# Cutting the attention output of a head pair in two halves of 512 queries on GpSimd

## What is computed

```python
def fox_attend(q, k, v, cq, ck, q_pos, k_pos):
    s = jnp.einsum('bqhd,bkhd->bhqk', q, k) * (1.0 / math.sqrt(HEAD_DIM))
    decay = cq_transposed[..., :, None] - ck_transposed[..., None, :]
    s = jnp.where(mask, s + decay, -inf)
    p = jax.nn.softmax(s, axis=-1)
    return jnp.einsum('bhqk,bkhd->bqhd', p, v)

o = attend(q).reshape(B, T, D_MODEL)
h = h + o @ w_o[l]
h = h + sq_relu_mlp(h, g_mlp[j], w_up[j], w_down[j])
```

## Time and profile before

| | |
|---|---|
| median of 3 runs | 2430.94 us (2430.47 to 2437.22) |
| the profiled execution | 2431.78 us, span 2430.0 us |
| TensorE busy | 2277.4 us, 94% of the span |
| VectorE busy | 1083.5 us, 45% |
| ScalarE busy | 584.0 us, 24% |
| GpSimd busy | 607.9 us, 25% |
| attention of the prompt | about 1290 to 1580 us from the span's start |
| output projection | 1580 to 1672 us |
| last MLP | 1672 us to near the end |

### The profile page before, as it was taken

The page is one execution under the profiler, slowest core; times in us unless marked ns, Lnnn a source line. Parts: engine busy times, 40 slices in busy tenths (PEclk is TensorE's granted clock), DMA queues, the critical chain, the costliest instruction groups (busy, mean ns, idle before and its releaser), DMA issues. The chain is left out here.

```text
span 2430.0 us, 35893 instructions
## 1 busy us (share of the span) xinstructions
PE 2277.4 (94%) x14058; PEld 2081.0 (86%) x14058; DVE 1083.5 (45%) x1757; ACT 584.0 (24%) x1257; POOL 607.9 (25%) x416
## 2 busy tenths in 40 slices
PE   3179999999999999999999999899999999999998
PEld 2179999999999996777776666699999999999997
DVE  5874343343343376544125777734424324334331
ACT  3142011011011043333214666622201101101101
POOL 1053223222322351210000110245223322322331
PEclk6589999999999999999998999999999999999999
DMA  4011111111111122544337454311111111111112
GB/s 122 0 30 44 52 45 44 45 53 44 45 47 49 37 86 83 174 137 122 132 131 185 110 121 98 78 35 44 52 45 44 47 51 44 44 47 50 44 44 80
DMA packets 194086, 169.14 MB, mean 70 GB/s; under 512 B 28560, under 2 KB 168896, under 8 KB 193927
## 3 DMA queue, kind: packets, MB, share of 16 engines
q1 hardware_dynamic: 152985, 136.92, 19.5%
q10 hardware_dynamic: 40950, 30.02, 3.9%
HBM read 136.77 MB, written 30.50 MB: 69 GB/s over the span
## 5 line engine op out<-in xcount | busy, mean ns | idle before, releaser
L322 PE MATMUL ps<-xn_hi,w_lo 128*128 128x352 f32 x1584 | 515.5, 325 | 62.8 <-DVE h L1859 39.4
L322 PE MATMUL ps<-xn_lo,w_hi 128*128 128x352 f32 x1584 | 510.1, 322 | 0.0
L322 PE MATMUL ps<-xn_hi,w_hi 128*128 128x352 f32 x1584 | 509.8, 322 | 0.0
L551 PE MATMUL ps<-hid_hi,w_lo 128*128 128x352 f32 x1536 | 495.4, 323 | 0.0
L551 PE MATMUL ps<-hid_lo,w_hi 128*128 128x352 f32 x1536 | 492.7, 321 | 0.0
L551 PE MATMUL ps<-hid_hi,w_hi 128*128 128x352 f32 x1536 | 492.2, 320 | 0.0
L300 POOL CAST w_hi<-w_raw 128x1024 fp32r<-128x1024 f32 x138 | 144.8, 1049 | 1136.3 <-issue 529.4
L621 DVE TENSOR_TENSOR h<-ps,h 128x352 f32<-128x352 f32 x384 | 198.3, 522 | 446.4 <-PE ps L551 446.4
L589 ACT ACTIVATE tmp_b<-tmp_a 128x352 f32<-128x352 f32 x192 | 95.3, 498 | 1090.6 <-DVE tmp_a L607 1090.6
L322 PEld LDWEIGHTS ps<-xn_hi,w_lo 128*128 128x128 f32 x1584 | 299.1, 189 | 66.5 <-DVE xn_lo L1853 39.6
L302 POOL TENSOR_TENSOR w_lo<-w_raw,w_hi 128x1024 fp32r<-128x1024 f32 x138 | 332.8, 2412 | 11.1
(11 more groups left out here) (211 smaller groups left out, 2489.1 us busy)
## 6 DMA issues: line engine op xcount, KB each, us to landing
w_raw<-in_w_up SPq DMA_DIRECT2D x64, 512.0 KB, 4.0
w_raw<-in_w_down SPq DMA_DIRECT2D x64, 512.0 KB, 3.4
out<-tok_out ACTq DMA_DIRECT2D x32, 256.0 KB, 2.2
qk_dram<-turn_hi ACTq DMA_DIRECT2D x32, 256.0 KB, 2.4
qk_dram<-turn_lo ACTq DMA_DIRECT2D x32, 256.0 KB, 2.9
k_page<-in_cache_k SPq DMA_DIRECT2D x32, 256.0 KB, 3.3
v_page<-in_cache_v SPq DMA_DIRECT2D x16, 512.0 KB, 9.0
q_a<-qk_dram SPq DMA_DIRECT2D x32, 256.0 KB
```

The lines of the kernel that those rows point to most:

```text
L322: last = pe.matmul(ps[:, bank, 0:CH], w, x(k, c), start=(k == 0 and i == 0), stop=(k == nk - 1 and i == 2))
L551: last = pe.matmul(ps[:, NC * (dm % 2) + c, 0:CH], w, x, start=(k == 0 and i == 0), stop=(k == GT - 1 and i == 2))
```

## The change

A pair is cut in two halves of 512 queries. `cut_o_pair(r, g)` waits until both heads have their half g in `oT`: 8 r copies of the pairs before, and 6 of this pair for the first half (two halves of the first head, one of the second) or 8 for the second. Each half raises `o_cut` by two, so pairs now raise it by 4, and all cuts together by 34. Chunk 0 of the first block of the projection reads columns 0 to 351 only, and waits ahead of k for the first half of pair k. Chunk 1 waits once for all cuts. The two weight splits stay ahead of pair 7.

```diff
                         elif par == 0 and c == 0:
-                            before = lambda k: pe.wait_ge(o_cut, 2 + 2 * (k + 1))
+                            before = lambda k: pe.wait_ge(o_cut, 2 * (2 * k + 1) + (2 if k else 0))
+                        elif par == 0 and c == 1:
+                            pe.wait_ge(o_cut, 4 * NP + 2)
                         last = products(pe, par, 0, KT, c, NC * par + c, oh, ol,
...
-            def cut_o_pair(r):
-                pool.wait_ge(o_ev, 8 * (r + 1))
-                cut_o(r + 1 if r else 0, r, slice(0, T))
-
-            cut_o_pair(0)
+            def cut_o_pair(r, g):
+
+                pool.wait_ge(o_ev, 8 * r + 6 + 2 * g)
+                cut_o(2 * r + g + (1 if r else 0), r, slice(512 * g, 512 * g + 512))
+
+            cut_o_pair(0, 0)
+            cut_o_pair(0, 1)
             pool.wait_ge(s_oc, 16)
             pool.tensor_copy(o_hi[:, :, T:N], o_s[:, :, :]).then_inc(o_cut, 1)
-            pool.wait_ge(o_cut, 3)
+            pool.wait_ge(o_cut, 5)
             pool.tensor_tensor(o_lo[:, :, T:N], o_s[:, :, :], o_hi[:, :, T:N].bitcast(F32), ALU.subtract).then_inc(o_cut, 1)
-            for r in range(1, NP - 1):
-                cut_o_pair(r)
-            split_one(pool, n_of["o"])
-            split_one(pool, n_of["o"] + 1)
-            cut_o_pair(NP - 1)
+            for r in range(1, NP):
+                if r == NP - 1:
+                    split_one(pool, n_of["o"])
+                    split_one(pool, n_of["o"] + 1)
+                cut_o_pair(r, 0)
+                cut_o_pair(r, 1)
```

## The result

| | before | after |
|---|---|---|
| median (first comparison, 6 runs each) | 2430.82 us (2430.23 to 2437.22) | 2420.46 us (2417.20 to 2422.91) |
| median (second comparison, 17 and 5 runs) | 2431.69 us | 2420.46 us (2417.65 to 2424.93) |
| the profiled execution | 2431.78 us, span 2430.0 | 2419.63 us, span 2417.9 |
| TensorE / VectorE / GpSimd busy | 2277.4 / 1083.5 / 607.9 us | 2276.1 / 1073.3 / 610.5 us |
| projection starts at | 1579.94 us | 1568.14 us |

The ratio is 0.9949 with a 95% interval of 0.9937 to 0.9961 in the first comparison and 0.9954 (0.9941 to 0.9967) in the second: 10 to 12 us faster, beyond the 0.3% that this kernel's measurement can tell. GpSimd is as busy as before. VectorE's busy time fell by 10.2 us: its 16 scalings over 128x896 alone, 7 of which had been stopped, fell from 24.8 to 14.2 us.

A forecast was written before the change was run, and what follows sets the result against it. Attention was taken as bound by its loop's latest link, TensorE waiting on VectorE scalings stopped by GpSimd. Savings 7.95 + 2.6 + 1.0 + 0.8 = 12.35 us off 2431.78 gave 2419.4 us, range 2417 to 2425.

The forecast's parts named there:

- pairs 1 to 5: Attention heads with these cuts: halving saves the whole 1.59 us per cut, 7.95 us in all.
- pair 0: Attention head with this cut: saves 2.6 us, of which 1.0 us for a lower TensorE clock behind the stall.
- pair 6: Attention head with this cut and the weight splits: saves 1.0 us, the middle of bounds 0 and 1.98 us.
- first halves: New GpSimd bursts in heads without a cut: VectorE's small scaling goes ahead of the subtraction, cost 0.
- The bound and the reading of it: Attention: GpSimd's whole cuts stop VectorE's scaling over 128x896, so TensorE's transposes wait 10.3 us in 7 events.
- Half sizes: GpSimd instructions over 512 columns: subtraction 1.27 us, cast 0.57 us.
- Second halves: Cut where wholes were: scaling stopped only to 1519.46, ending 1519.94 us; ScalarE's pT copies come next, covering the cut.
- What a whole cut cost: Attention: a head with a cut takes 18.02 us, one without 16.43, so one cut costs 1.59 us.
- Rival 1: First half's subtraction stops the small scaling: 0.5 us seven times, 3.5 to 4 us lost, 2423.1 us; chance 0.10.
- The end: Start of the projection: TensorE's wait for pair 7's cut goes, saving 0.8 us, bounds 0.5 and 0.9.
- Rivals 2 and 3: Uncut heads only catch up: no change, 2431.0 us, chance 0.10; halves take as long as wholes: 2438 us, chance 0.06.

The follow-up runs named there:

- e3: The changed kernel, but both halves of a pair are cut only once the whole pair is in oT; 2421.46 us, ratio 0.9954.
- e4: All cuts of oT wait for the last copy, so attention has no cut beside it; 2453.83 us, only the heads are read.
- e7: As e6, plus sample columns cut in the gap of head 2 and weight blocks split in halves in later gaps; 2419.43 us, ratio 0.9943.
- e6: The changed kernel, but second halves of pairs 0 to 6 wait for a longer gap between VectorE's scalings; 2421.51 us, ratio 0.9948.
- e8: The changed kernel, but both halves of pair 0 wait for the whole pair; 2420.28 us, ratio 0.9959.
- e11: The kernel before, unchanged, run once more for a second profile; 2435.64 us.
- e10: The kernel before, plus two small GpSimd MEMSETs in head 1 that nothing reads; 2431.51 us, ratio 1.0001.
- e1: The kernel before, with only pair 7 in halves and the projection's chunks waiting accordingly; 2434.06 us, ratio 1.0001.
- e2: The changed kernel, but chunk 0 of the projection waits for both halves of each pair and chunk 1 for nothing; 2418.92 us, ratio 0.9944.
- e5: The kernel before, with whole cuts of pairs 0 to 6 moved into a longer gap between VectorE's scalings; 2434.61 us, ratio 1.0004.
- e9: The kernel before, with only pair 0 in halves, the first as early as it can go; 2431.88 us, ratio 0.9994.
- r1: The changed kernel run again unchanged, to see how much of its profile repeats; 2420.46 us, ratio 0.9954.

## Why the prediction was right

Predicted 2419.4 us in 2417 to 2425, measured 2420.46: the mechanism is right; the terms of pairs 1 to 5 and of pair 0 are too large, that of pair 6 is too small, and the first halves cost nothing by another way than forecast. By its steps:

- **The bound and the reading of it.** That TensorE's 7 waits are VectorE's stops by GpSimd: shown, since the waits go when the instructions are halved (e3) and when no cut stands beside the scalings (e4, e7).
- **Half sizes.** The subtraction took 1.27 us, as the line between two sizes gave. The cast took 0.61 and not 0.57.
- **Second halves.** The scaling ended 1.15 us after its start (1.10 forecast), and ScalarE's `pT` was next, as said: the transposes wait 0.53 us for it, as long as in the same heads of e4, where nothing is cut.
- **What a whole cut cost.** This term was mis-sized: 1.59 us were taken against the head after it, but the two heads of a pair differ by about 0.13 us with no cut near (e4, e7). The right floor is 16.56 us, the cost 1.47, and five pairs give 7.34 for 7.95. The forecast of 16.4 us in every head was wrong for the same reason, and so was my e6.
- **First halves.** Cost 0, right. The way there was wrong: the prediction had the small scaling stopped by the end of the cast and the subtraction held back behind it. In all seven heads the scaling began 0.1 us before the recorded end of the cast and took 0.29 us, as alone, and the subtraction began before the scaling's recorded end and took its 1.27 or 1.28 us. Rival 1 did not come.
- **Pair 0.** 2.00 us for 2.6. After the change 17.06 us remain, since the cut of the sample columns meets the scaling over 128x1024 (1.31 us long, 0.75 alone); cut later (e3, e8) or placed elsewhere (e7), they leave 16.56 or 16.57. The prediction left their cut as it was but let the head fall to 16.43. Of the 2.00, 0.5 belongs to the lower clock of that one profile: in e11, e10 and e1 the same head took 18.57 to 18.61, so a usual saving is 1.5. That the clock would not fall was right for both profiles of the change.
- **Pair 6.** 1.51 us for 1.0, which was the middle of wide bounds and no calculation. The prediction had the weight splits meet other scalings; they meet the same ones as before (0.96, 0.47 and 1.71 us long in both kernels), because the first of them is held by the scaling over 128x896 and starts in the same place relative to VectorE. 0.33 us over the floor stays.
- **The end.** The wait is gone; from the 1st to the 36th matmul of the projection it takes 5.67 and 5.68 us in the two profiles of the change (and 5.67 in e1) for 6.49 in both of the kernel before, so it was worth 0.82 us for 0.8. What follows varies from profile to profile by as much: the whole stretch to the end took 849.76 and 849.15 us after, 850.06 and 850.90 before. Which chunk waits for what was not needed for it (e2).
- **Rivals 2 and 3** fall by e4 and by the 1.27 us.

The sum of what the theory holds is 7.34 + 1.5 + 1.51 + 0.8 = 11.2 us with pair 0 at its usual saving, for the 12.35 forecast, beside a difference of the medians of 10.4 and 11.2. The profiled pair differs by 12.1 and would have made the prediction look better than it was: 1.6 of it are the stretch between heads 1 and 2. That 2420.46 lies only 1 us from the forecast is in part luck: 0.6 us too much at pairs 1 to 5 and 0.6 to 1.1 at pair 0 stand against 0.5 too little at pair 6 and against a stretch that the sum did not have. How much of that stretch is in the medians no profile says.

On the rule of the Trainium skill, "SBUF — State Buffer", that the shared port pair is locked for one whole instruction: e3 agrees, in that the waiting VectorE comes in at the end of one subtraction, ahead of the next cast, in seven of seven pairs. The page's restart of about 115 ns was measured with VectorE ahead and GpSimd waiting. Taken for the other direction, and with the whole instruction of 0.69 us behind it, as the prediction tried, it would have made 1.47 us of the 1.15; what had been stopped ends 0.49 us after GpSimd does (1511.16 less 1510.67), not 0.81. And the small scaling beside the end of a cast was not lengthened at all, which a lock held up to the end as recorded would not allow. In both the measurement decides.

## What to carry to other kernels

If an engine that is idle nearly always stops a busy one for the length of an instruction, cut its instructions until the stop fits into the slack of the place; its total work and its share of the span say nothing about it. Look for such stops as a few instructions of a group that are much longer than the rest of the same shape, and price them by the distance of one instruction between repeats of the loop, against the same phase of the loop without the stop, not against the neighbouring one. A whole instruction moved to a place with a longer gap but no slack (e5) won nothing that the times show, while halves at the old place (e3) won it all.

## What had not been expected of the hardware

Between heads 1 and 2 TensorE does 96 small matmuls for a sample unit (L1222, with 32 columns of weights each) and then, in eight of the fourteen profiles, has a hole in which it waits for nothing that the profile shows. The loads of weights just behind it, in the kernel before, its second profile e11, the change, e8 and e3 in this order:

```profile
1327.80 0.86 PEld L1422 LDWEIGHTS ps<-ident,p_hi 128*128 128x128 f32 x8 [1.79 <-issue]
```

```profile
1329.68 1.31 PEld L1422 LDWEIGHTS ps<-ident,p_hi 128*128 128x128 f32 x8 [3.12 <-issue]
```

```profile
1326.81 0.86 PEld L1424 LDWEIGHTS ps<-ident,p_hi 128*128 128x128 f32 x8 [0.20 <-issue]
```

```profile
1325.25 0.85 PEld L1424 LDWEIGHTS ps<-ident,p_hi 128*128 128x128 f32 x8 [0.20 <-issue]
```

```profile
1326.06 0.86 PEld L1424 LDWEIGHTS ps<-ident,p_hi 128*128 128x128 f32 x8 [2.06 <-issue]
```

In all seven profiles with whole cuts of pairs 1 to 6 (before, e1, e4, e5, e9, e10, e11) the stretch takes 25.98 to 29.74 us; in six of the seven with halves (the change, r1, e2, e6, e7, e8) it takes 24.39 or 24.40, and in e3 26.27. e3 has the same instructions on every engine as the change and differs in the numbers that GpSimd waits for. What stands beside the hole are the loads of `q`, `k` and `v` of the next head (length; busy time of the five engines with their counts; granted clock, DMA share, GB/s), here in the kernel before:

```profile
1320.00:1325.00 5.00, 4.54 (x82) 3.00 (x86) 2.86 (x9) 3.21 (x10) 0.00 (x0) 1.00 1.07 249
1325.00:1330.00 5.00, 3.45 (x50) 2.56 (x50) 0.66 (x3) 1.75 (x4) 0.00 (x0) 1.00 0.18 36
1330.00:1335.00 5.00, 5.00 (x107) 2.69 (x105) 2.09 (x8) 1.55 (x5) 0.00 (x0) 1.00 0.02 5
```

|---|---|---|---|
| kernel before | 1324.98 to 1326.30 | 1326.00 | 1327.80 |
| e11 | 1327.02 to 1328.21 | 1326.56 | 1329.68 |
| e3 | 1323.10 to 1324.42 | 1324.00 | 1326.06 |
| the change | 1317.12 to 1318.08 | 1326.61 | 1326.81 |
| r1 | 1319.96 to 1321.17 | 1325.12 | 1325.33 |

In all eight profiles with a hole (all seven with whole cuts, and e3) TensorE goes on 1.4 to 1.6 us after such a packet has landed, wherever that falls; in all six without one the packet had landed 4.0 us or more before. So the hole fits instructions that arrive late, and its end follows the packet. That is a match in fourteen profiles and not an experiment: no run moved the packet alone, and the profile doesn't say whose instructions it holds. Why it comes earlier in nearly all kernels with halves stays open: an op of GpSimd at that time was tried (e8, e9, e10) and is not it. The stretch takes 24.39 to 29.74 us over all profiles; up to 2.9 of the 5.3 us between are the hole, and the rest is the clock.

The granted clock fell to 0.50, the lower level, for about 3 us or more behind some holes of TensorE and not behind others of the same length: in the kernel before behind one of the seven stops and not behind the 1.8 us between heads 1 and 2, in e11 behind none of the stops but behind those 3.1 us (from 1330 to 1333 us). It did not fall behind 2.1 us in e3 and fell behind 1.5 us in e4. Such a fall cost 0.5 us at pair 0 of the kernel before, 1.0 to 1.3 in e5, and 1.5 to 2.5 between heads 1 and 2 (e1, e4, e5, e9, e10, e11), on top of the hole. During the heads each of the seven profiles with whole cuts has at least one fall, and of the seven with halves only e6 has one, at its weight splits. The two profiles of the kernel before differ by 3.9 us, and 2.95 of it is the stretch between heads 1 and 2, hole and clock together; that its times lie near 2431 and near 2435 us may come from this, but two profiles don't show it.
